# Hybrid decoder step on one core: in the delta rule's inversion the inverse and the first product change partition halves, so that a level's products use four array quarters

## The reference

```python
low = jnp.where(strict, jnp.einsum('nbhid,nbhjd->nbhij', kb, kc) * decay, 0.0)
t_inv = lax.linalg.triangular_solve(eye + low, jnp.broadcast_to(eye, low.shape), left_side=True, lower=True)
u = jnp.einsum('nbhij,nbhjd->nbhid', t_inv, vc * bc[..., None])
w = jnp.einsum('nbhij,nbhjd->nbhid', t_inv, kb * jnp.exp(G)[..., None])
```

## Time and profile before

| | us |
|---|---|
| median of 3 runs | 1251.15 |
| the three runs | 1251.51, 1251.15, 1248.06 |
| profiled execution, first to last instruction (span) | 1246.8 |
| delta rule's inversion, `turn_T` to `last_p` | 225.7 to 254.6 |
| expert loop | 319.6 to the end |

### The profile page before, as it was taken

One profiled execution on the slowest core, in us unless ns is written; L12 is line 12 of the kernel. 1 busy time (PEld: TensorE's weight loads), 2 busy tenths in 40 slices (PEclk: granted clock), 3 DMA queues, 4 the chain that ended last, 5 costly groups with the idle time before them and its releaser, 6 DMA issues.

```text
span 1246.8 us, 18342 instructions
## 1 busy us (share of the span) xinstructions
PE 1196.7 (96%) x7340; PEld 516.0 (41%) x7340; DVE 444.9 (36%) x937; ACT 228.7 (18%) x389; POOL 94.9 (8%) x173
## 2 busy tenths in 40 slices
PE   8998998999999999999999999999999999999996
PEld 6765665875333333333333333323332333333332
DVE  3575826537431331322231322313132222231324
ACT  3312257235020101101020101101010101020202
POOL 6213312611000000000000000000000000000000
PEclk9998999999999999999999999999999999999999
DMA  9788971419999999999999999999999999999994
GB/s 323 283 337 295 331 253 37 152 33 392 369 400 421 414 428 428 426 427 427 426 427 428 428 426 429 428 429 426 428 428 429 427 427 428 429 426 428 428 425 168
DMA packets 66590, 464.34 MB, mean 372 GB/s; under 512 B 18510, under 2 KB 18510, under 8 KB 38758
## 3 DMA queue, kind: packets, MB, share of 16 engines
q1 hardware_dynamic: 65336, 446.59, 87.1%
q0 software_dynamic: 1152, 16.78, 3.4%
q10 hardware_dynamic: 46, 0.18, 0.1%
HBM read 459.82 MB, written 3.70 MB: 372 GB/s over the span
## 4 chain that ended last, share of the span: by engine, by line
PE 63%; DMA 19%; ACT 1%; DVE 1%; issue 1%; SPq 0%; DVEq 0%; ACTq 0%
PE bank L2291 22%; DMA ring<-in_w_up 19%; PE bank L2306 9%; PE bank L2326 8%; PE bank L2248 4%; PE bank L2227 4%; PE bank L1570 2%; PE bank L2231 1%; PE bank L2252 1%; PE bank L1361 1%; PE bank L1422 1%; PE bank L2353 1%; PE bank L1432 1%; PE bank L1435 1%; PE bank L2334 1%
## 5 line engine op out<-in xcount | busy, mean ns | idle before, releaser
L2291 PE MATMUL bank<-ring,work 128*64 128x512 f32 x1056 | 244.5, 605 | 17.3 <-DMA ring<-in_w_up 17.3
L2326 PE MATMUL bank<-ring,work 128*64 128x512 f32 x736 | 162.8, 594 | 3.0 <-ACT work L2423 3.0
L2291 PEld LDWEIGHTS bank<-ring,work 128*64 128x64 f32 x1056 | 76.7, 139 | 178.9 <-issue 151.0
L513 PE MATMUL bank<-hoT,ring 128*128 128x288 f32 x448 | 116.2, 416 | 5.6 <-DMA ring<-in_w_in 4.8
L2479 DVE TENSOR_TENSOR Xw<-Xw,bank 128x512 f32<-128x512 f32 x64 | 43.8, 688 | 213.6 <-PE bank L2248 213.6
L2291 PE MATMUL bank<-work 128*64 128x512 f32 x256 | 113.1, 595 | 0.0
L2413 ACT ACTIVATE work<-bank 128x1024 f32<-128x1024 f32 x16 | 16.4, 1025 | 491.4 <-PE bank L2231 463.7
L2306 PE MATMUL bank<-ring,work 128*64 128x512 f32 x448 | 106.3, 595 | 0.0
L2291 PE MATMUL bank<-hoT,work 128*64 128x512 f32 x224 | 99.1, 595 | 0.0
L513 PEld LDWEIGHTS bank<-hoT,ring 128*128 128x128 f32 x448 | 85.2, 194 | 31.5 <-issue 7.8
L2326 PEld LDWEIGHTS bank<-ring,work 128*64 128x64 f32 x736 | 51.6, 137 | 102.0 <-issue 101.0
(11 more groups left out here) (429 smaller groups left out, 1307.9 us busy)
## 6 DMA issues: line engine op xcount, KB each, us to landing
ring<-in_w_up SPq DMA_DIRECT2D x94, 2048.0 KB, 24.9
ring<-in_w_down SPq DMA_DIRECT2D x28, 2048.0 KB, 26.9
work<-in_w_up SPq DMA_DIRECT2D x19, 2048.0 KB, 20.8
ring<-in_w_down SPq DMA_DIRECT2D x36, 1024.0 KB, 26.5
hoT<-in_w_up SPq DMA_DIRECT2D x15, 2048.0 KB, 25.1
work<-in_w_down SPq DMA_DIRECT2D x9, 2048.0 KB, 25.1
ring<-in_cache_v SPq DMA_DIRECT2D x64, 256.0 KB, 5.0
hoT<-in_w_down SPq DMA_DIRECT2D x8, 2048.0 KB, 29.9
```

The source lines that it names most:

```text
L513: ins = pe.matmul(bank[:, i % 2, 0:T], w[:, k, :], hT[:, k, :], start=k == 0, stop=k == KD - 1)
L2291: ins = pe.matmul(bank[CAP * e:CAP * e + CAP, g, :], xT[:, k, CAP * e:CAP * e + CAP], weight(c0 + ch + e, k % 2 * RSLOT + 512 * g), start= ...
L2326: ins = pe.matmul(bank[CAP * e:CAP * e + CAP, 4 + m, :], aT[:, k, CAP * e:CAP * e + CAP], weight(c0 + ch + e, k % 4 * D + 512 * m), start= ...
```

## The change

The inverse `Tb` and the product `Y` are kept in the other partition half than `Lm` and `TT`. `turn_T` makes besides the transpose also a copy of `Tb` in the other half, by a product with `I64` on the left, and DVE copies it back over `Tb` (three copies more, and d_T counts one more for each group). Then the product for TT reads half 1-a and writes half a, the product for Tb reads and writes half 1-a, and their loops are merged into one, so that the two alternate. With a = 0 and 1 these are all four quarters. Four waits are new: group B of `turn_T` waits for the last `d_QK` and group D for the second `s_wor`, since their new products go to banks 7 and 3, and `level_p` of level 1 and the product of group D wait for DVE's copy of group D.

```diff
+        X_BANK = {"A": (5, 0), "B": (7, 0), "D": (3, 0)}
...
                     if g == "B":
                         pe.wait_ge(s_wor, 1)
+                        pe.wait_ge(d_QK, 5)
+                    if g == "D":
+                        pe.wait_ge(s_wor, 2)
                     for u, a in units(g):
-                        ins = pe.matmul(unit(Y_BANK, g, u, a), ub(Tb, u, a), I64[pr(a), :], start=True, stop=True)
+                        pe.matmul(unit(Y_BANK, g, u, a), ub(Tb, u, a), I64[pr(a), :], start=True, stop=True)
+                        ins = pe.matmul(unit(X_BANK, g, u, 1 - a), I64[pr(a), :], ub(Tb, u, a), start=True, stop=True)
                     ins.then_inc(d_Tr, 1)
...
-                        ins = pe.matmul(unit(Y_BANK, g, u, a), ub(Lm, u, a), ub(TT, u, a), start=True, stop=True)
+                        ins = pe.matmul(unit(Y_BANK, g, u, 1 - a), ub(Lm, u, a), ub(TT, u, a), start=True, stop=True)
...
                 def level_p(g, l):
                     pe.wait_ge(d_Ye[g], l)
-                    pe.wait_ge(d_T[g], l)
+                    pe.wait_ge(d_T[g], l + 1)
                     if l == 1:
                         pe.wait_ge(s_wor, PARTS)
                         pe.wait_ge(s_kun, 5)
+                        pe.wait_ge(d_T["D"], 2)
                     for u, a in units(g):
-                        ins = pe.matmul(unit(T_BANK, g, u, a), ub(Tb, u, a), ub(Y, u, a), start=True, stop=True)
-                    ins.then_inc(d_PT[g], 1)
-                    for u, a in units(g):
-                        ins = pe.matmul(unit(P_BANK, g, u, a), ub(Y, u, a), ub(Tb, u, a), start=True, stop=True)
+                        ins = pe.matmul(unit(T_BANK, g, u, a), ub(Tb, u, 1 - a), ub(Y, u, 1 - a), start=True, stop=True)
+                        if (u, a) == units(g)[-1]:
+                            ins.then_inc(d_PT[g], 1)
+                        ins = pe.matmul(unit(P_BANK, g, u, 1 - a), ub(Y, u, 1 - a), ub(Tb, u, 1 - a), start=True, stop=True)
                     ins.then_inc(d_P[g], 1)
...
+                for i, g in enumerate(GRP):
+                    dve.wait_ge(d_Tr, i + 1)
+                    dve.tensor_copy(Tb[:, cols(g)], pb(X_BANK, g)).then_inc(d_T[g], 1)
                 for l in range(1, LAST):
```

More of the change, by code:

```diff
@@ L1440, in last_y @@
                     for u, a in units(g):
-                        ins = pe.matmul(unit(Y_BANK, g, u, a, LO, LO), ub(Lb, u, a, HI, LO), ub(TT, u, a, HI, HI),
+                        ins = pe.matmul(unit(Y_BANK, g, u, 1 - a, LO, LO), ub(Lb, u, a, HI, LO), ub(TT, u, a, HI, HI),
                                         start=True, stop=True)
@@ L1446, in last_p @@
                     pe.wait_ge(d_Ye[g], LAST)
-                    pe.wait_ge(d_T[g], LAST)
+                    pe.wait_ge(d_T[g], LAST + 1)
                     for u, a in units(g):
-                        ins = pe.matmul(unit(P_BANK, g, u, a, LO, LO), ub(Tb, u, a, LO, LO), ub(Y, u, a, LO, LO),
+                        ins = pe.matmul(unit(P_BANK, g, u, a, LO, LO), ub(Tb, u, 1 - a, LO, LO), ub(Y, u, 1 - a, LO, LO),
                                         start=True, stop=True)
@@ L1463, in _ @@
                         pe.wait_ge(d_Ye["D"], 1)
+                        pe.wait_ge(d_T["D"], 2)
                         for u, a in units("D"):
-                            ins = pe.matmul(unit(T_BANK, "D", u, a), ub(Tb, u, a), ub(Y, u, a), start=True, stop=True)
+                            ins = pe.matmul(unit(T_BANK, "D", u, a), ub(Tb, u, 1 - a), ub(Y, u, 1 - a), start=True, stop=True)
                         ins.then_inc(d_PT["D"], 1)
```

## The result

| | kernel before | changed kernel |
|---|---|---|
| median of the runs | 1249.86 us (20 runs) | 1252.72 us (20 runs) |
| ratio, 95% interval | 1 | 1.0022 [1.0015, 1.0029] |
| profiled span | 1246.8 | 1250.7 |
| `turn_T` starts | 225.67 | 228.05 |
| from there to `make_u` | 28.97 | 32.14 |

A time 6.6 us lower was forecast; it became 2.8 us higher (0.0022 x 1250; the interval is 1.9 to 3.6). So times are counted from this start.

What follows compares the result with a forecast made beforehand. The weight stream waits for the last chunk's state, whose chain in the inversion is TensorE alone. Level savings and tail, 2.01 + 1.78 + 1.52 + 1.67 - 0.41 = 6.57 us, off 1251.15 gave 1244.6 us; 8-in-10 range 1241.0 to 1250.0.

Steps and rivals of the forecast that it cites:

- What bounds the kernel: Expert loop's weight stream waits for the last chunk's state; a microsecond less in the inversion counts one for one.
- The instructions must also come fast enough: Four quarters need 14.6 ns for a matmul and its load; L1441 does 16.3 ns, 10% short of the need.
- something that may go: Before L1474, PE stood 0.64 us for nothing the profile shows; this stop may go too.
- Nothing changes: In `turn_T`, 160 matmuls at 14.6 ns last as long as 80 at 29.2, 2.33 us; waits and copies cost nothing.
- A level: In the inversion, level 2 takes 3.82 us instead of 5.60, levels 3 and 4 take 4.08 each.
- The term of the products: In a level, each group's merged 64 matmuls take 0.93 us instead of 1.87, 14.6 ns for one.
- the end of a level: From the start of A's products to TT of A being ready for the next Y, 1.95 us.
- DVE, not PE, as the last before Y: Sign in levels 3 and 4, 4.1 us from Y to Y: Y waits last for DVE.
- POOL's masks: POOL needs 4.75 us a level, more than 4.08, but its lead leaves 0.5 us to spare at level 4.
- instructions or starts don't keep up: Four quarters' matmuls start slower than 14.6 ns: 1247.8 us at 20 ns, 1251.2 at 25; chance 0.12.
- Rivals 2 and 3: 2: four quarters no faster than two, 1254.2 us, chance 0.06; 3: quarters sharing rows take turns, 1273.8 us, chance 0.04.
- The fourth: PE's clock behind or in the inversion: one fall more or less is 1.8 us; beyond that, chance 0.05.

Runs made afterwards that it cites:

- full_loop: The changed kernel with PE's levels 1 to 4 of groups A and B as one hardware loop, group D's work moved behind; ratio to the kernel before 0.9956.
- after_loop: The changed kernel with levels 2 to 4 as a hardware loop on PE, level 1 ahead of it; ratio to the kernel before 0.9982.
- pad_cold: The changed kernel with 40 increments of an unused semaphore on PE between the products of A and B in each level; ratio to the kernel before 1.0220.
- before_loop: The kernel before with levels 2 to 4 as a hardware loop on PE, level 1 ahead of it; ratio to the kernel before 0.9997.
- two_full_loop: full_loop with a level's two products in two loops again, so that two quarters work at a time; ratio to the kernel before 1.0006.
- turn_alone: The kernel before with `turn_T`'s second product alone, its result unused, levels as before; ratio to the kernel before 1.0009.

## Why the prediction was wrong

- **What bounds the kernel** held. The stream stands until the last state is there, and the time follows that state to within about 1 us: in full_loop it is 5.6 us earlier and the time 5.5 us less (0.0044 x 1250), in after_loop 1.2 and 2.3, in pad_cold 27.1 later and 27.5 more, in the changed kernel 1.8 later and 2.8 more.
- **"The instructions must also come fast enough"** is the step that failed. I took 16.3 ns for a matmul from 64 of L1441. Those are 128 instructions in 1.23 us, half a block, which TensorE had in stock. A short burst says nothing of a supply that is refilled 256 at a time. The rows that would have told are the counts over the whole inversion. Stretches of the kernel before, its inversion and what follows up to the store of the state:

```profile
225.67:254.70 29.03, 28.59 (x1009) 28.20 (x1009) 13.39 (x21) 9.34 (x18) 17.68 (x12) 1.00 0.21 66
...
254.64:272.33 17.69, 17.05 (x494) 16.28 (x491) 5.08 (x12) 4.68 (x9) 0.00 (x0) 0.90 0.02 4
```

  2018 instructions in 29.03 us, 14.4 ns each; the supply gives one in 15.0 when it sets the pace, and some 500 were in stock at the start (in every kernel with a first stop it comes 504 recorded instructions after `turn_T`'s start, the semaphores' among them). The kernel before stood close to this second bound (before_loop, which is freed of it in levels 2 to 4, gains 0.0003 in the ratio), and its one stop, the 0.64 us ahead of L1474, was the sign of it: it stands at the same count as a stop of the changed kernel, 256 x 6 behind the first one. I listed it as something that may go. I also had 29.2 ns for a matmul as the pace of two quarters; the supply's is 30, and I didn't ask whether the two are different things. They are: two_full_loop's levels have no supply to wait for, and its loads still start 29.2 ns apart.
- **`turn_T`: "Nothing changes."** The array's part was right, 160 matmuls in 2.33 us as forecast. But they are 160 instructions more with their loads, 160 x 15.0 = 2.4 us of supply. turn_alone shows this part by itself: `make_u` 3.0 us later. And the blocks came no sooner for `turn_T`'s faster use of them: instruction 2040 after its start runs at 29.68 us in the kernel before and at 30.23 in the changed one, which still has 160 to go. Part of this is the late first packet, whose cause is open.
- **A level** was right wherever instructions weren't short: 4.28, 4.25 and 4.05 us in full_loop against 3.82, 4.08 and 4.08. The term of the products held, 14.6 ns for a matmul. What was too small is the end of a level: from the first product's load to the next level's Y 2.25 us (239.52 to 241.77) against 1.95, the 0.40 us of the loop's branch in it. The sign "DVE, not PE, as the last before Y" did not show: full_loop's chain names PE and "issue" there. In the changed kernel all 6.6 us of it were lost, since the blocks' arrival, not the array, sets when its 2181 instructions are through.
- **POOL's masks** were not late in full_loop: PE's waits from 230 to 254 us name no POOL.
- **The rivals.** The first, "instructions or starts don't keep up", was the one, but I put it in nanoseconds between starts and priced it from better than nothing to no change, at most 1251.2 us (r = 25 ns). As a rate over blocks it is worse: the four quarters can't gain anything, and the 160 instructions are a loss. Rivals 2 and 3 are refuted by the 14.6 to 15.4 ns. The fourth was at work as well, with the sign that hid the loss: the granted clock behind the inversion was 0.90 in the profile of before (row above; PE had stood idle for parts of the 3 us ahead of it) and 1.00, the higher of the two levels (2.4 GHz), in the one of after, where this part lasted 16.28 instead of 17.69 us. So 1.4 of the 3.2 us that the inversion lost are not seen at the state. The changed kernel from `make_u` on, to a little beyond the state:

```profile
260.19:277.50 17.31, 16.72 (x520) 15.60 (x515) 5.09 (x12) 5.27 (x10) 0.00 (x0) 1.00 0.02 4
```

- **What stays open:** why turn_alone, whose `make_u` is as late as the changed kernel's, costs 1.1 us and not 2.8 in the time. Their intervals overlap (up to 1.0021, from 1.0015), they come from different sets of runs, and the stops vary by some tenths from kernel to kernel. Open, too, is what holds the first packet.

The change as made should not be kept by itself. With PE's four levels as a loop it is worth 5.5 us by the ratio, 0.9956 [0.9940, 0.9972] (3.5 to 7.5 us), and 4.0 us by the medians of the same set, 1244.57 against 1248.53. The variants with DVE's swap can't be told from it (0.9953, 0.9954 and 0.9968, intervals of about the same width). The old two-quarter kernel with all four levels as a loop was not run; nearest are before_loop (0.9997) and two_full_loop (1.0006). What is left of the supply there is one stop of 1.9 us in level 1.

## What to carry to other kernels

Before making an engine's instructions shorter or more, divide the time of the stretch by all its instructions on that engine, weight loads included, over more than a few hundred: near 15 ns on TensorE the supply is the next bound, and unexplained "issue" time inside a run of like instructions, 256 apart, is its sign. Straight-line repetition of small matmuls is then what to remove, by a hardware loop whose body is brought once, and two changes that are each worth nothing (loop 0.9997, four quarters 1.0022) can be worth something together (0.9982 with the same loop over levels 2 to 4, 0.9956 with all four levels in it).

## What the runs showed that I had not expected

- TensorE gets straight-line instructions in blocks of 256 (16 KB), one in 3.6 to 4.0 us when it is short of them: 15 ns for one instruction, 30 ns for a matmul with its load. The next packet starts only 1.1 to 1.2 us after PE enters a block (2.97 in the first, among other transfers) and is used 2.4 to 2.8 us after its start. A loop body of 384 matmuls and loads stays in place: in full_loop no instruction packet of TensorE's starts from level 2 to the loop's end; in the three loops with DVE's swap a single one does, 12.9 to 13.5 us after `turn_T`'s start, and PE does not stop there.
- Four 64 x 64 quarters, two by two sharing rows, do work at once: one matmul in 14.6 ns over 128 by the starts of the loads.
- An increment of a semaphore as an instruction of its own costs TensorE 0.15 us (6.0 us for 40) in the middle of matmuls.
- The granted clock over a level fell to 0.64 to 0.81 where 40 increments, 6 us of an idle array, stood in each; in full_loop's levels, with no pause of over 0.4 us, it was 1.00.
